# Head groups of a windowed attention: the second pass over the scores is made again by TensorE with keys on partitions, in place of transposing the exponentials

## The chip, the cores and the metric

One core of one Trainium2 chip runs the whole layer as one program. The metric is the device time of one execution in microseconds; lower is better. All data are fp32 in HBM; products that need two operands split into a high and a low part run in the fp32r format, the others in full fp32.

## The reference, cut to what matters

The layer has an attention over 1024 latent tokens with 8 query heads and 2 key/value heads (4 query heads share one key/value head), head width 64. A block of 128 queries reads one softmax over a per-head sink logit, 256 context keys and the latent keys within 128 positions.

```python
s_loc = jnp.einsum("bqhgd,bkhd->bhgqk", qb, kb).astype(jnp.float32) * scale
s_loc = jnp.where(valid, s_loc, NEG_INF)
s_ctx = jnp.einsum("bqhgd,bkhd->bhgqk", qb, k_ctx).astype(jnp.float32) * scale
p = jax.nn.softmax(jnp.concatenate([sink_col, s_ctx, s_loc], axis=-1), axis=-1)
o = (jnp.einsum("bhgqk,bkhd->bqhgd", p[..., 1:1 + n_ctx], v_ctx)
     + jnp.einsum("bhgqk,bkhd->bqhgd", p[..., 1 + n_ctx:], vb))
```

Beside it there is a Conformer convolution (31 taps, 512 channels) with a layer norm, and a vector `mod = silu(c) @ w_mod + b_mod`, of which sections 2 to 5 are needed only after the attention. The attention's and the convolution's outputs feed `w_out`; then comes the gated MLP.

## The kernel before, in words

The program is two blocks one after the other. The first makes the norms, the input projection, the convolution and the attention; the second makes the output projection and the MLP. Each engine has its queue written out by hand in program order, and semaphores join them.

The input projection for queries, keys and values runs over `NK` = 10 tiles of 128 tokens (2 of context, 8 latent). Queries and keys are normed and rotated on DVE, split into a high and a low half (`qst`, `kst`) and transposed by TensorE (`turn_qk`), so that the 128 partitions hold 64 high and 64 low rows of a query, and a key's high (or low) part twice. One product of a query with the key's high part and one with its low part give the exact score. The key is scaled by its inverse norm (`k_scaled`); the query's inverse norm `msq` is not put into the query but into the exponential's `scale`.

The attention runs over `NGRP` = 16 head groups n, each a block of 128 queries (i = n // 2) times one key/value head (4 query heads). A group has 5 key tiles of 128 keys (2 context, 3 latent), and 4 at the two edges (groups 0, 1, 14, 15). So there are 76 items (n, j). The scores and maxima run one group ahead of the rest, and a group goes so:

- `scores(n + 1, hl)` on TensorE, one head at each of the first four items of group n: queries on partitions, 640 keys along the columns; a context product of 256 columns with the high and one with the low key part, the same for two latent tiles, a mask by an identity product, and the third latent tile likewise with its mask: 8 products for a head of an inner group. It waits for the exponential of the head two before, which frees its two PSUM banks.
- `maxima` on DVE: `reduce_max` over 640 columns (L1274) and a small `tensor_scalar` (L1277) that scales it and takes the sink in.
- `exps` on ACT (L990): exponential of 640 columns, with the sum of a row into `accum_out`.
- `turn(n, j)` on TensorE (L728): four transposes of 128 x 128, one for each head, into bank 4 or 5.
- ACT copies that bank to SBUF (`pt`, L1059).
- `values(n, j - 1)` on TensorE (L740): two full-fp32 products of 256 columns, one for even and one for odd heads, each writing 64 of the 128 PSUM partitions of bank 6.
- `denominators` on DVE (sum plus sink, reciprocal of 4 columns), `spread` on TensorE (L752: four products that lay the reciprocals out over 64 partitions), a copy on ACT (L1068), and one multiplication on DVE (L1419) that ends the group.

Around this stand the convolution's taps on DVE (`taps`, `join_taps`, groups 1 to 9), the layer norm (groups 10 to 15, with TensorE's `mean`, `variance`, `broadcast`, `column_sums` in `beside`), the split of `w_out` (`WO_HIGH`, `WO_LOW`), and the second modulation on GpSimd: for 8 row blocks and 4 sections it multiplies a loaded 128 x 1024 piece of `w_mod` by a column (L546) and adds it into `sums` by an accumulating DMA (L554). GpSimd starts this after the last transposed key or query is placed (`qkT_out`). `row_sums` (L800) are the last products of the block.

## Time and profile before

| what | value |
|---|---|
| median of 3 runs | 1178.93 us (1176.92 to 1184.31) |
| profiled execution | 1178.23 us; span 1176.4 us, mean granted TensorE clock 0.988 |
| TensorE busy in the span | 1114.9 us (95%) |
| DVE, ACT, POOL busy | 935.4, 581.5, 288.0 us |
| HBM traffic | 113.26 MB read, 30.41 MB written |

The span runs from the first to the last profiled instruction; the execution's own time is 1.8 us longer. An engine's busy share is an average over stages with different limits, so the stage of the head groups (about 228 to 422 us from the span's start) is read by itself below. A matmul's own duration contains its pipeline's depth; what it costs in a stream is the distance from its start to the next one's start.

### The profile page before, as it was taken

Reading aid. Unit: us, or ns where it says so; the run is one execution under the profiler, and the core shown is the slowest. Engines: PE = TensorE matmul, PEld = TensorE weight load, DVE = VectorE, ACT = ScalarE, POOL = GpSimd, SP = SyncE. Lnnn points to the kernel's source line nnn. Section 1 sums busy time; section 2 is a strip of 40 time slices with the busy share of each in tenths; the row PEclk is TensorE's granted clock in tenths of the full one; section 3 lists DMA queues with packets and bytes.
Section 4 is the critical chain, followed back from the end, with each engine's and each line's share of the span. In section 5 each row is a group of like instructions: output and inputs, shape, how many; then the busy total and the mean of one; then the engine's idle time right before and its main releaser. Section 6 shows DMA issues by size and latency. Waiting matters only on the chain.

```text
span 1176.4 us, 16722 instructions
## 1 busy us (share of the span) xinstructions
PE 1114.9 (95%) x5745; PEld 908.1 (77%) x5745; DVE 935.4 (80%) x1430; ACT 581.5 (49%) x1007; POOL 288.0 (24%) x329
## 2 busy tenths in 40 slices
PE   7899999889878899998899999999999999999998
PEld 7787888767656677876688888878888878888886
DVE  0679988787988664469999999999999875868776
ACT  1662356865646775555443434343534444444442
POOL 2200111134464000002545544555520020000010
PEclk9999999998999899999999999999999999999999
DMA  9422556629999315222445353545342375354354
GB/s 365 163 80 73 119 107 118 151 48 257 255 243 270 93 55 178 91 77 84 147 140 180 125 181 128 178 134 178 116 152 74 123 260 196 107 118 133 99 132 109
DMA packets 103089, 171.74 MB, mean 146 GB/s; under 512 B 9323, under 2 KB 62691, under 8 KB 102005
## 3 DMA queue, kind: packets, MB, share of 16 engines
q1 hardware_dynamic: 83540, 106.79, 27.6%
q0 software_dynamic: 19488, 64.17, 22.5%
q8 instruction: 35, 0.57, 0.2%
q14 instruction: 26, 0.20, 0.1%
HBM read 113.26 MB, written 30.41 MB: 122 GB/s over the span
## 4 chain that ended last, share of the span: by engine, by line
PE 42%; DVE 12%; issue 5%; ACT 4%; DVEq 0%; ACTq 0%
PE ps L1711 19%; PE ps L1761 6%; PE ps L1763 6%; PE ps L1762 6%; PE ps L1676 5%; DVE y L2127 2%; DVE w_op L2028 2%; DVE w_raw L2046 1%; DVE y L2123 1%; ACT y L1920 1%; ACT w_op L1832 1%; DVE u L2116 1%; DVE s_sum L2046 1%; ACT h_second L1825 0%; PE ps L1687 0%
## 5 line engine op out<-in xcount | busy, mean ns | idle before, releaser
L1711 PE MATMUL ps<-t_op,w_op 128*128 128x512 f32 x1056 | 247.7, 390 | 3.8 <-DVE cv L2116 2.1
L1711 PEld LDWEIGHTS ps<-t_op,w_op 128*128 128x128 f32 x1056 | 197.5, 188 | 48.1 <-issue 4.9
L1711 PE MATMUL ps<-hx,w_op 128*128 128x512 f32 x792 | 189.5, 392 | 8.8 <-DVE u L2116 6.1
L1711 PEld LDWEIGHTS ps<-hx,w_op 128*128 128x128 f32 x792 | 149.1, 189 | 42.1 <-DVE u L2116 6.2
L1832 ACT ACTIVATE w_op<-w_raw 128x512 fp32r<-128x512 f32 x132 | 79.9, 623 | 195.0 <-DVE w_raw L2046 191.1
L1761 PE MATMUL ps<-dnh,ah 128*128 128x512 f32 x308 | 120.1, 390 | 1.6 <-DVE dnl L2134 1.6
L1763 PE MATMUL ps<-dnh,al 128*128 128x512 f32 x308 | 119.8, 389 | 0.0
L1762 PE MATMUL ps<-dnl,ah 128*128 128x512 f32 x308 | 119.8, 389 | 0.0
L2028 DVE TENSOR_TENSOR w_op<-w_raw,w_op 128x512 fp32r<-128x512 f32 x132 | 101.5, 783 | 10.1 <-ACT w_op L1832 8.5
L1940 ACT ACTIVATE ah<-hid 128x512 fp32r<-128x512 f32 x77 | 48.6, 632 | 116.8 <-PE ps L1763 112.7
L2134 DVE TENSOR_TENSOR al<-hid,ah 128x512 fp32r<-128x512 f32 x77 | 53.2, 691 | 46.3 <-ACT ah L1940 45.8
L2278 POOL DMA_DIRECT2D wd<-in_w_down x44 | 32.0, 728 | 236.2 <-DVE h_first L2017 162.2
L1676 PE MATMUL ps<-wo_op,hx 128*128 128x512 f32 x336 | 79.4, 392 | 0.3 <-PEq L350 0.3
L1676 PEld LDWEIGHTS ps<-wo_op,hx 128*128 128x128 f32 x336 | 62.4, 188 | 14.1 <-issue 1.1
L1761 PEld LDWEIGHTS ps<-dnh,ah 128*128 128x128 f32 x308 | 57.8, 188 | 14.3 <-DVE dnl L2134 2.4
L1763 PEld LDWEIGHTS ps<-dnh,al 128*128 128x128 f32 x308 | 57.8, 188 | 12.1
L1762 PEld LDWEIGHTS ps<-dnl,ah 128*128 128x128 f32 x308 | 57.8, 188 | 11.9
L740 PE MATMUL ps<-pt,vraw 128*64 128x256 f32 x304 | 49.9, 412 | 16.9 <-ACT pt L1059 16.8
L2284 POOL TENSOR_TENSOR wd<-wd 128x256 f32<-128x256 f32 x44 | 46.4, 1055 | 76.6 <-DMA wd<-in_w_down 74.9
L990 ACT ACTIVATE p<-ps,scal,msq 128x640 f32<-128x640 f32 (+1 forms) x60 | 51.8, 864 | 27.0 <-DVE scal L1277 25.4
L1274 DVE TENSOR_REDUCE scal<-ps 128x1 f32<-128x640 f32 (+1 forms) x64 | 50.0, 782 | 16.8 <-PE ps L711 10.7
L1059 ACT ACTIVATE pt<-ps 128x512 f32<-128x512 f32 x76 | 44.9, 592 | 21.0 <-PE ps L728 20.6
(294 smaller groups left out, 2369.4 us busy)
## 6 DMA issues: line engine op xcount, KB each, us to landing
w_raw<-in_w_up SPq DMA_DIRECT2D x44, 512.0 KB, 5.0
wm<-in_w_mod SPq DMA_DIRECT2D x32, 512.0 KB, 6.2
sums<-wm POOLq DMA_DIRECT2D x32, 512.0 KB, 8.4
wd<-in_w_down POOLq DMA_DIRECT2D x44, 256.0 KB, 3.3
w_down_sums<-wd POOLq DMA_DIRECT2D x44, 256.0 KB, 2.8
dn_raw<-w_down_sums SPq DMA_DIRECT2D x44, 256.0 KB, 2.6
hid_scratch<-hid SPq DMA_DIRECT2D x20, 512.0 KB, 4.3
hid<-hid_scratch POOLq DMA_DIRECT2D x20, 512.0 KB, 5.4
```

The source lines that it names most:

```text
L740: last = pe.matmul(ps[a * HD:(a + 1) * HD, 6, 0:2 * P], vraw[:, kts[j], g, :], pt[:, it % NPT, :].rearrange("p (r a q) -> p a r q", r=2, a ...
L990: act.activation(probs(n)[:, hl, 0:w], score_ap(hh, w), ACT.Exp, scale=msq[:, CT + n // NG, GQ * (n % NG) + hl:GQ * (n % NG) + hl + 1], bi ...
L1274: dve.reduce_max(s[:, 0, hl:hl + 1], score_ap(hh, w), axis=AX.X, negate=True).then_inc(max_done, 1)
L1676: last = pe.matmul(ps[:, b + hh, :], a, wo_half(k, lo, hh), start=(k == 0 and v == 0 and lo == 0), stop=(k == KT - 1 and v == 1))
L1711: last = pe.matmul(bank_of(p, s), w_op[p][w][:, k, :], rows_of(p, k, v), start=(start and k == 0 and w == 0 and v == 0), stop=(k == KH - 1 ...
L1761: pe.matmul(o, ah[b][:, c_], dnh[b][:], start=start, stop=False, skip_group_check=True)
L1762: pe.matmul(o, ah[b][:, c_], dnl[b][:], start=False, stop=False, skip_group_check=True)
L1763: return pe.matmul(o, al[b][:, c_], dnh[b][:], start=False, stop=(i == NK2 - 1), skip_group_check=True)
L1832: act.activation(w_op[p][0][:], w_part(s, p), ACT.Copy).then_inc(up_hi, 1)
L1940: act.activation(ah[n % 3][:], down_rows(p, i), ACT.Copy).then_inc(dn_hi, 1)
L2028: dve.tensor_tensor(out=w_op[p][1][:], in0=w_part(s, p), in1=f(w_op[p][0][:]), op=ALU.subtract).then_inc(up_lo, 1)
L2134: dve.tensor_tensor(out=lo[n % 3][:], in0=src, in1=f(hi[n % 3][:]), op=ALU.subtract).then_inc(dn_split, 1)
```

## The change

- The first pass over the scores is made only for the row maxima: `scores` leaves out the low part of the keys (5 products in place of 8 for a head of an inner group) and waits for the maximum of the head two before, not for its exponential.
- A second pass, `turned_scores(n, j)`, takes the transposes' place: the 128 keys of a tile are stationary, the 4 heads' queries (512 columns) move, once with the key's high and once with its low part; a masked tile has one more product of 512 columns; and a last one of 512 columns adds minus the row maximum (`onesr` stationary; `shift`, a diagonal of 128 x 128 for each head, moving).
- ACT makes the exponential of those 512 columns straight into `pt`; the exponentials of 640 columns, their accumulated sums and the copies of `pt` are gone.
- `values` comes two items later (`LAG` = 2), and makes the sums of the exponentials by two more full-fp32 products of 256 columns with `ones` as the stationary operand, into columns 256 to 511 of the same bank; the sink's term goes in by four small products at a group's last item. `spread` and `rden`'s copy are gone.
- `normalized(n)` on DVE: a reciprocal of 256 columns from PSUM, and the multiplication. It stands at item j = 1 of the next group. `shifts(n + 1)` on DVE makes the minimum with the sink, the diagonal (512 columns) and the sink's argument at item 3; `maxima` loses its small second instruction. The bank of the output alternates between 6 and 7 for groups 3 to 9 (`out_bank`).
- In the tiles of the input projection each latent tile's queries are scaled by `msq` on DVE (`q_scaled`, 512 columns) before the split.
- GpSimd starts the second modulation after the last tile of the input projection (`qkv_mm`), with `sums` at another place in SBUF; the places of `w_out`'s halves are permuted, and ACT no longer waits for the modulation before the first of them.

```diff
-        sums = [at(kib, f"sums{a}", [P, D]) for a, kib in enumerate((83, 87, 91, 95))]
-        pbuf = [at(119, "p0", [P, GQ, SW]), at(129, "p1", [P, GQ, SW])]
+        sums = [at(kib, f"sums{a}", [P, D]) for a, kib in enumerate((123, 127, 131, 135))]
+        shift = at(119, "shift", [P, 2, GQ, P], F32R)
+        neg_max = at(17.75, "neg_max", [P, 2, GQ], F32R)
+        onesr = at(17.25, "onesr", [P, P], F32R)
...
-        WO_KIB = ((57, 61), (65, 69), (99, 103), (73, 77), (81, 85), (89, 93), (107, 111))
+        WO_KIB = ((81, 85), (89, 93), (99, 103), (73, 77), (57, 61), (65, 69), (107, 111))
...
+        def out_bank(n):
+            return 7 if n % 2 and 3 <= n < LN else 6
+
+        LAG = 2
+        item_of = [(n, j) for n in range(NGRP) for j in range(len(key_tiles(n // NG)))]
...
-                pool.wait_ge(qkT_out, len(items))
+                pool.wait_ge(qkv_mm, NK)
...
                     if hh >= 2:
-                        pe.wait_ge(exp_done, hh - 1)
+                        pe.wait_ge(max_done, hh - 1)
...
-                    pe.matmul(ps[:, b, 0:CTX], q, kTc[:, g, 0, :], start=True, stop=False)
-                    pe.matmul(ps[:, b, 0:CTX], q, kTc[:, g, 1, :], start=False, stop=True)
-                    o = ps[:, b, CTX:CTX + 2 * P]
-                    pe.matmul(o, q, kl[0][:, lat:lat + 2 * P], start=True, stop=False)
-                    last = pe.matmul(o, q, kl[1][:, lat:lat + 2 * P], start=False, stop=False)
+                    pe.matmul(ps[:, b, 0:CTX], q, kTc[:, g, 0, :], start=True, stop=True)
+                    last = pe.matmul(ps[:, b, CTX:CTX + 2 * P], q, kh[:, lat:lat + 2 * P], start=True, stop=False)
...
-                    for hl in range(GQ):
-                        last = pe.transpose(ps[:, pt_bank(it), hl * P:(hl + 1) * P], probs(n)[:, hl, j * P:(j + 1) * P], ident[:])
-                    last.then_inc(pt_T, 1)
...
+                        pe.wait_ge(exp_done, it - 1)
+                    o = ps[:, st_bank(it), :].rearrange("p (h q) -> p h q", h=GQ)
+                    q = hx[:, GQ * g:GQ * (g + 1), 0, i * P:(i + 1) * P]
+                    for v in range(2):
+                        if kt < CT:
+                            k_ = kTc[:, g, v, kt * P:(kt + 1) * P]
+                        else:
+                            k_ = hx[:, 2 * g + v, 1, (kt - CT) * P:(kt - CT + 1) * P]
+                        pe.matmul(o, k_, q, start=(v == 0), stop=False)
+                    if kt >= CT and kt - CT != i:
+                        mask = mask_prev if kt - CT < i else mask_next
+                        pe.matmul(o, mask[:], identr[:].unsqueeze(1).to_broadcast([P, GQ, P]), start=False, stop=False)
+                    if j == 0:
+                        pe.wait_ge(shift_done, n + 1)
+                    pe.matmul(o, onesr[:], shift[:, n % 2], start=False, stop=True).then_inc(st_mm, 1)
...
+                    if j == 0 and n:
+                        pe.wait_ge(o_norm, n if out_bank(n - 1) == b else n - 1)
...
+                    pe.wait_ge(exp_done, it + 1)
+                    first, end = (j == 0), (j == len(kts) - 1)
+                    if end:
+                        pe.wait_ge(sexp_done, n + 1)
+                        for hl in range(GQ):
+                            r, a = divmod(hl, 2)
+                            pe.matmul(ps[a * HD:(a + 1) * HD, b, (2 + r) * P:(3 + r) * P], st[n % 2][:, 3, hl:hl + 1].to_broadcast([P, HD]), ident[:],
+                                      start=False, stop=False, skip_group_check=True)
+                    probs = pt[:, it % NPT, :].rearrange("p (r a q) -> p a r q", r=2, a=2)
+                    for c_, w in enumerate((vraw[:, kts[j], g, :], ones[:, 0:HD])):
+                        for a in range(2):
+                            last = pe.matmul(ps[a * HD:(a + 1) * HD, b, 2 * c_ * P:2 * (c_ + 1) * P], w, probs[:, a],
+                                             start=first and c_ == 0, stop=end, skip_group_check=True)
                     last.then_inc(pv_mm, 1)
...
+                def exps(it):
+                    act.wait_ge(st_mm, it + 1)
+                    if it >= NPT:
+                        act.wait_ge(pv_mm, it - NPT + 1)
+                    act.activation(pt[:, it % NPT, :], ps[:, st_bank(it), :], ACT.Exp).then_inc(exp_done, 1)
...
+                    if m >= CT:
+                        q3 = h3(qa[:, m % 2, :])
+                        dve.tensor_tensor(out=q3, in0=q3, in1=msq[:, m, 0:NH].unsqueeze(2).to_broadcast([P, NH, HD]), op=ALU.mult).then_inc(q_scaled, 1)
...
+                def shifts(n):
...
+                    dve.tensor_tensor(out=neg_max[:, n % 2], in0=s[:, 0, :], in1=sinks[:, 1, GQ * g:GQ * (g + 1)], op=ALU.min).then_inc(negm_done, 1)
+                    dve.wait_ge(negm_done, n + 1)
+                    dve.tensor_tensor(out=shift[:, n % 2], in0=ident[:].unsqueeze(1).to_broadcast([P, GQ, P]),
+                                      in1=f(neg_max[:, n % 2]).unsqueeze(2).to_broadcast([P, GQ, P]), op=ALU.mult).then_inc(shift_done, 1)
+                    dve.tensor_tensor(out=s[:, 3, :], in0=sinks[:, 0, GQ * g:GQ * (g + 1)], in1=f(neg_max[:, n % 2]), op=ALU.add).then_inc(arg_done, 1)
...
+                def normalized(n):
+                    b = out_bank(n)
+                    dve.wait_ge(pv_mm, first_item[n + 1])
+                    dve.reciprocal(rden[:], ps[:, b, 2 * P:4 * P]).then_inc(den_done, 1)
+                    dve.wait_ge(den_done, n + 1)
+                    if n:
+                        dve.wait_ge(o_lo, n)
+                    dve.tensor_tensor(out=on[:], in0=ps[:, b, 0:2 * P], in1=rden[:], op=ALU.mult).then_inc(o_norm, 1)
```

## Rows read from the trace of the kernel before

**Rows 1.** The page, part 2: tenths of TensorE's full clock in 40 slices of 29.4 us

```profile
PEclk9999999998999899999999999999999999999999
```

**Rows 2.** Windows: busy us (x instructions) of PE, PEld, DVE, ACT, POOL; clock; DMA

```profile
226.00:250.00 24.00, 19.08 (x142) 15.18 (x141) 16.12 (x43) 18.17 (x42) 0.00 (x0) 0.86 0.27 94
...
300.00:325.00 25.00, 22.23 (x179) 16.38 (x179) 22.68 (x42) 14.72 (x34) 11.59 (x13) 1.00 1.02 250
325.00:350.00 25.00, 17.93 (x146) 12.70 (x146) 22.15 (x37) 14.23 (x31) 15.89 (x13) 1.00 1.00 243
```

**Rows 3.** Timeline of DVE (start us, us): ends of groups 1 and 12

```profile
252.84 0.42 DVE L1419 TENSOR_TENSOR on<-ps,rden 128x256 f32<-128x256 f32 x1
...
392.90 0.42 DVE L1419 TENSOR_TENSOR on<-ps,rden 128x256 f32<-128x256 f32 x1 [0.16 <-PE ps L740]
```

**Rows 4.** Waits, 226 to 426 us: us in total, times, longest

```profile
ACT p L990 <- DVE scal L1277: 25.4, 32, 2.6
PEld ps L740 <- ACT pt L1059: 23.0, 16, 4.1
...
PEld ps L698 <- ACT p L990: 9.8, 18, 1.5
```

**Rows 5.** Timeline of PE: one head's scores, four transposes, two value products

```profile
301.98 0.36 PE L698 MATMUL ps<-kTc,hx 128*128 128x256 f32 x1
302.19 0.28 PE L699 MATMUL ps<-kTc,hx 128*128 128x256 f32 x1
302.30 0.29 PE L701 MATMUL ps<-hx 128*128 128x256 f32 x1
...
302.54 0.22 PE L704 MATMUL ps<-mask_prev,identr 128*128 128x128 f32 x1
302.60 0.28 PE L709 MATMUL ps<-hx 128*128 128x128 f32 x1
...
302.83 0.28 PE L711 MATMUL ps<-mask_next,identr 128*128 128x128 f32 x1
302.94 0.63 PE L728 MATMUL ps<-ident,p 128*128 128x128 f32 x4
303.50 0.65 PE L740 MATMUL ps<-pt,vraw 128*64 128x256 f32 x4
304.08 0.39 PE L698 MATMUL ps<-kTc,hx 128*128 128x256 f32 x1
```

**Rows 6.** Timeline of PE in the input projection: an fp32r product of 512 columns

```profile
150.73 0.40 PE L826 MATMUL ps<-qwh,hx 128*128 128x512 f32 x1
150.96 0.28 PE L827 MATMUL ps<-qwh,hx 128*128 128x256 f32 x1
```

**Rows 7.** Timeline of PE: full-fp32 products late in the stage, and its end

```profile
411.66 0.66 PE L752 MATMUL ps<-ident,scal 128*64 128x128 f32 x8
412.14 1.03 PE L740 MATMUL ps<-pt,vraw 128*64 128x256 f32 x8
413.11 1.09 PE L728 MATMUL ps<-ident,p 128*128 128x128 f32 x8
414.58 1.94 PE L791 MATMUL ps<-ones,sums 128*128 128x32 f32 x16 [0.38 <-DVE cacc L1300]
...
421.95 3.70 PE L800 MATMUL ps<-sums,ones 128*128 128x512 f32 x8
```

**Rows 8.** Timeline of PE: where the first and the second group start

```profile
230.95 1.09 PE L728 MATMUL ps<-ident,first_probs 128*128 128x128 f32 x4 [2.19 <-DVE ka L1209]
...
241.48 0.39 PE L698 MATMUL ps<-kTc,hx 128*128 128x256 f32 x1
```

**Rows 9.** DVE by source line: ns min/median/max, first and last start us, forms

```profile
L1993 DVE RECIPROCAL scal<-scal x8: 164/164/165, 452.0 to 527.9; 128x1 f32<-128x1 f32 x8
L1293 DVE RECIPROCAL scal<-scal x1: 195/195/195, 405.0 to 405.0; 128x8 f32<-128x8 f32 x1
L1260 DVE TENSOR_TENSOR qst<-qa,qst x8: 681/683/693, 167.7 to 240.2; 128x512 fp32r<-128x512 f32 x8
```

**Rows 10.** Lines, 226 to 426 us: busy us, mean ns of one | idle before

```profile
L1277 DVE TENSOR_SCALAR scal<-scal,msq,sinks 128x1 f32<-128x1 f32 x60 | 16.4, 273 | 2.2
```

More of the change, by code:

```diff
@@ L736, in values @@
                     if j == 0 and n == 0:
                         pe.wait_ge(qkT_out, IN_GROUPS)
-                    pe.wait_ge(pt_out, it + 1)
-                    for a in range(2):
-                        last = pe.matmul(ps[a * HD:(a + 1) * HD, 6, 0:2 * P], vraw[:, kts[j], g, :],
-                                         pt[:, it % NPT, :].rearrange("p (r a q) -> p a r q", r=2, a=2)[:, a],
-                                         start=(j == 0), stop=(j == len(kts) - 1), skip_group_check=True)
@@ L743, in values @@
-                    last.then_inc(pv_mm, 1)
-                def spread(n):
-                    pe.wait_ge(den_done, 2 * n + 2)
-                    if n < 2:
-                        pe.wait_ge(qkT_out, IN_GROUPS + 3 * (n + 1))
-                    bank_read(n)
-                    for hl in range(GQ):
-                        r, a = divmod(hl, 2)
-                        last = pe.matmul(ps[a * HD:(a + 1) * HD, 7, r * P:(r + 1) * P], st[n % 2][:, 2, hl:hl + 1].to_broadcast([P, HD]), ident[:],
-                                         start=(r == 0), stop=True, skip_group_check=True)
-                    last.then_inc(r_mm, 1)
+                    if j == 0 and b == 7:
+                        pe.wait_ge(qkT_out, len(items))
@@ L846, in _ @@
                         beside(n, j)
-                        if j == OUT_AT(n):
-                            spread(n)
-                        if j:
-                            values(n, j - 1)
-                    values(n, m - 1)
+                        if first_item[n] + j >= LAG:
+                            values(first_item[n] + j - LAG)
+                for it in range(len(item_of) - LAG, len(item_of)):
+                    values(it)
                 for r in range(2):
@@ L1010, in beside @@
                     if k is not None:
-                        if k == 0:
-                            for a in range(NW):
-                                act.wait_ge(mod_acc[a], 16 * KT)
-                        elif k > 1:
+                        if k > 1:
                             act.wait_ge(ln_mm, 4 if k == 2 else 6)
@@ L1023, in _ @@
                         placed += 1
-                    if m == NK - 2:
-                        for hl in range(2):
-                            exps(0, hl)
                     read_tile(m)
@@ L1034, in _ @@
                         product(act)
-                        for hl in range(2, GQ):
-                            exps(0, hl)
                         place(placed)
@@ L1341, in _ @@
                             maxima(0, hl)
+                        shifts(0)
                     square_sums(m)
@@ L1364, in _ @@
                     i, g, kts = head_steps(n)
-                    s = st[n % 2]
-                    dve.wait_ge(negm_done, GQ * (n + 1))
-                    dve.tensor_tensor(out=s[:, 3, :], in0=sinks[:, 0, GQ * g:GQ * (g + 1)], in1=s[:, 1, :], op=ALU.add).then_inc(arg_done, 1)
                     for j in range(len(kts)):
@@ L1370, in _ @@
                             maxima(n + 1, j)
+                            if j == GQ - 1:
+                                shifts(n + 1)
+                            if n and j == 1:
+                                normalized(n - 1)
                             if n == 0 and j == 0:
@@ L1410, in _ @@
                             wo_split_low(dve, WO_LOW[n, j])
[L1411 to L1413 removed]
+                        if n == NGRP - 1 and j == 1:
+                            normalized(n - 1)
+                        if n and j == 3:
                             output_low(n - 1)
[L1415 to L1419 removed]
+                normalized(NGRP - 1)
                 modulation()
```

101 lines of the change are left out of this document (29 added, 72 removed).

## The prediction

> **What bounds the kernel now.** I read the clock's strip first: it is at full speed nearly everywhere, with dips inside the attention stage [rows 1]. Then the stage by windows: TensorE is busy 22.2 of 25 us in one window and 17.9 in the next, DVE 22.7 and 22.2, and ACT and GpSimd are far below [rows 2]. At the start the clock is 0.86, after TensorE has sat idle. So neither TensorE nor DVE is full, and the waits say why: ACT's exponential waits for DVE's scaled maximum (25.4 us in all), TensorE's values for ACT's copy of `pt` (23.0 us on the weight loads alone), and its scores for the exponential (9.8 us) [rows 4]. It is a ring through three engines: scores, maximum, exponential, next scores. Last, the pace: group 1 ends at 252.84 and group 12 at 392.90, so a group of five tiles takes 140.06 / 11 = 12.73 us [rows 3].
>
> How much of that is TensorE's own work? I go by distances from start to start. A head's scores: 301.98 to 302.94, 0.96 us. Four transposes: 302.94 to 303.50, 0.56. An item's values: 0.58 [rows 5]. The spread of the reciprocals: 411.66 to 412.14, 0.48 [rows 7]. A group: 4 x 0.96 + 5 x 0.56 + 5 x 0.58 + 0.48 = 10.0 us, plus 0.25 on the mean for the layer norm. So TensorE waits some 2.5 us of each group, a fifth. The question is whether what the change gives TensorE to do is less than what it frees.
>
> **TensorE, part by part.** First pass: an inner head keeps its first product (0.21), one more of 256 columns (0.12), a mask (0.06), one of 128 (0.11) and its mask (0.11): 0.61 us in place of 0.96 [rows 5]. An edge head keeps three: 0.39.
>
> Second pass: a tile takes 3 products of 512 columns (high, low, shift), and 4 where it is masked, 5 x 3 + 2 = 17 in a group of five tiles and 4 x 3 + 1 = 13 in one of four. An fp32r product of 512 columns takes 150.73 to 150.96, 0.23 us [rows 6]: 3.9 us, where the transposes took 2.8.
>
> Values: four full-fp32 products of 256 columns in place of two. The stretch at 412.14 has just these eight records (two items' worth) and lasts to 413.11: 0.97 us an item [rows 7], where it was 0.58. Even and odd heads write different halves of the array's columns and already run side by side, so the sums by ones queue behind the values. The sink's products are those of the spread, 0.45.
>
> A change of kind between the second pass and the values costs about 0.1: four transposes at 0.11 each (the step from 302.83 to 302.94) would be 0.44 and take 0.56 [rows 5]. In all 4 x 0.61 + 3.9 + 5 x 0.97 + 0.5 + 0.45 = 12.1 us a group, 12.4 with the layer norm. That is as long as the 12.73 us that a group takes now. **The waits go, and TensorE's own work takes their place.**
>
> **The whole stage.** From the start of group 1's first item to the end of the values TensorE has: first pass 48 x 0.61 + 8 x 0.39 = 32.4; second pass, 13 + 12 x 17 + 2 x 13 = 243 products x 0.23 = 55.9; values 74 x 0.97 = 71.8 (two items come over from group 0, as they now lag by two); changes of kind 74 x 0.1 = 7.4; sinks 16 x 0.45 = 7.2; three sets of key and query transposes, at 0.44 each, 1.3; the unchanged work beside, 8 records of 512 columns at (3.70 - 0.6) / 7 = 0.44 and 48 small ones at 0.12, 9.3 [rows 7]. Sum 185.3 us.
>
> Group 0: TensorE is held to 230.95 by DVE's rotation of the last tile, which frees a score bank, and this wait stays; from there to group 1 it takes 10.53 us [rows 8] for 6.6 us of work at full clock (three sets of transposes, four items of values, a spread, two heads, two key and query sets). The new work there is 10 x 0.23 + 2 x 1.07 + 2 x 0.39 + 0.9 = 6.1 us. With the same waits and slow clock, group 1 starts at 241.0, 0.5 earlier.
>
> So the values end at 241.0 + 185.3 = 426.3 if TensorE never waits, against 421.95 now (where L800 starts) [rows 7]. Waits that I expect to stay: where the output has one bank (groups 1, 2 and 11 to 15), the next values need the normalized output, which is a reciprocal and a multiplication after the last values, while TensorE has only a head and a second pass (0.61 + 0.92 = 1.5 us) to fill it; seven times 0.3. And the layer norm's mean and variance now stand behind the normalization in DVE's queue: 2 us in groups 11 and 12. Together about 4: the values end near 430, 8 us later than now.
>
> **DVE.** The reciprocal of 256 columns is in no row. One column takes 164 ns and eight 195 [rows 9]: 4.4 ns a column, so 164 + 255 x 4.4 = 1.29 us; the other end is the 0.42 us of the multiplication of the same width from PSUM [rows 3]. I take 1.29, since both reciprocals' rows set it. A group loses four L1277 at 0.27 [rows 10] and two small instructions, 0.35, and gets the minimum (0.16), the diagonal (0.68, as L1260 of that width) and the reciprocal in the small one's place: +0.7. At 22.68 of 25 us [rows 2] a group of taps costs it 10.5 to 11 us now, so 11.5: under TensorE's 12.1, with little left. The scaling of the queries is another 0.68 us for each of 8 tiles in the input projection; TensorE has no wait for DVE there, the transposes come a tile later, and I put it at nothing (if that cover failed, at most 8 x 0.68 = 5.4 us). The shift is ready a tile and a half before its product asks for it.
>
> The rule of the Trainium skill that speaks against this part is in "VectorE: DVE Perf Modes", First, the fixed hardware budget: the reciprocal is an iterative divide with a repeat count of 8. At eight of its cycles a column my estimate by that page would be 2.3 us, and the seven one-bank groups would wait a microsecond longer each; the rows' 4.4 ns a column are half of that.
>
> **ACT, GpSimd, DMA, the end.** ACT drops from about 7.5 to 4 us a group and bounds nothing; an item's exponential has two items of TensorE's work to hide in. The modulation on GpSimd starts some 20 us earlier and ends as much earlier; nobody waits for its end now (the column sums at 414.58 wait for DVE [rows 7]), so it is worth nothing, and its slowing of DVE only moves to earlier groups. At the end the reciprocal, the multiplication and two small instructions (2.1 us) lie under three `row_sums` of 0.9. Nothing there.
>
> Profiled execution 1178.2 (span 1176.4 and 1.8 around it), which is the median within 0.7. Plus 8: **1186 us**.
>
> **The rivals.**
> - **DVE sets the pace (slower).** Place: the normalization at item 1 of the next group, in DVE's queue behind taps and joins, or layer-norm work. It decides where reciprocal and multiplication end more than 1.5 us after the values. For it: DVE's 90% now, its +0.7, its stretched instructions beside GpSimd. Against: seven groups have two banks. With 1.5 us lost in each of the seven one-bank groups, where I took 0.3, and 0.5 in the other nine: +13, 1199. By the page's eight cycles it comes here too.
> - **Switches and the clock come out better (no change).** If no change of kind costs anything (-7.4) and group 0 is 2 us shorter because its waits go: 1177. For it: TensorE's queue is never dry now. Against: the 0.56 for four transposes.
> - **The sums by ones are nearly free (faster).** If the array ran them beside the values, 74 x 0.39 = 29 us less: 1157. Against: the 0.97 of rows 7, where four products of two items do follow one another.
> - **The waits don't go.** If TensorE still waited a tenth of its time, +18: 1204. For it: three engines still hang together through maximum, shift and normalization. Against: all of them have more than an item of lead.
>
> **How the numbers follow.** Chances: forecast 0.50 (1181 to 1193), DVE 0.17, better switches 0.17, free sums 0.07, waits stay 0.09. The range leaves out the free sums and the far end of the last: 1168 to 1205. A measurement of this kernel tells about 1% (12 us) from no change: faster than 1167, the free sums and a little, 0.09; slower than 1191, DVE, the waits and a tenth of the forecast, 0.31; within, 0.60.
>
> **What the profile of the changed kernel would show.** TensorE busy over 24 of each 25 us from 250 to 400; distances of 0.23 for the second pass and 0.97 for an item's values; the clock at 1.00; a group each 12.4 us; reciprocals of 1.3 us; ACT half idle, waiting for TensorE; the modulation's last DMA near 360. I am wrong if the group's pace is 11 us (a distance mis-sized), or if TensorE's waits for DVE add to over 10 us.

## The result, and the profile after

| | before | changed |
|---|---|---|
| median | 1177.93 us (4 runs beside the others) | 1206.55 us (4 runs) |
| ratio | | 1.0234, 95% interval 1.0183 to 1.0285 |
| start of the first projection product | 143.8 | 145.2 |
| last projection product | 226.4 | 229.0 |
| group 1 starts | 241.48 | 243.15 |
| `row_sums` start (the values have ended) | 421.95 | 449.26 |
| span | 1176.4 us | 1204.6 us |

The changed kernel is 28.6 us slower, outside my range of 1168 to 1205. (One of its four executions, 1298 us, had a lower clock throughout and is left out of the ratio, as is one of 1434 us of the first experiment.) The 27.3 us at `row_sums` are all but 0.9 us of the difference between the spans. Of them 1.7 are there when group 1 starts, and 25.6 come in groups 1 to 15.

The page of the changed kernel: the span, part 1, and part 2's clock, which answers to [rows 1]; below, ACT's exponentials in part 5.

```profile
span 1204.6 us, 16655 instructions
...
PE 1157.0 (96%) x5825; PEld 917.4 (76%) x5825; DVE 962.1 (80%) x1390; ACT 519.9 (43%) x861; POOL 289.7 (24%) x330
...
PEclk9999999899999999999999999999999999999999
...
L987 ACT ACTIVATE pt<-ps 128x512 f32<-128x512 f32 x76 | 45.4, 597 | 137.8 <-PE ps L736 137.8
```

ACT now waits 137.8 us for TensorE: the ring of before [rows 4] is cut, as meant. The windows of the changed kernel, columns as in [rows 2]:

```profile
250.00:275.00 25.00, 23.79 (x164) 15.29 (x164) 22.45 (x31) 6.77 (x14) 10.16 (x11) 1.00 1.04 261
275.00:300.00 25.00, 25.00 (x170) 15.55 (x168) 22.06 (x30) 6.77 (x14) 14.27 (x14) 1.00 1.04 263
300.00:325.00 25.00, 25.00 (x170) 15.85 (x170) 23.73 (x29) 6.84 (x14) 14.04 (x14) 1.00 1.05 260
325.00:350.00 25.00, 25.00 (x170) 15.66 (x168) 24.79 (x36) 6.92 (x14) 13.50 (x12) 1.00 1.03 252
350.00:375.00 25.00, 22.65 (x149) 14.10 (x145) 22.53 (x28) 5.88 (x13) 6.53 (x6) 1.00 0.79 214
375.00:400.00 25.00, 21.81 (x130) 12.96 (x128) 15.90 (x24) 8.80 (x17) 0.00 (x0) 0.93 0.00 1
400.00:425.00 25.00, 23.30 (x144) 14.57 (x144) 14.70 (x26) 8.96 (x15) 0.00 (x0) 0.93 0.07 22
425.00:450.00 25.00, 23.81 (x166) 15.70 (x167) 17.14 (x25) 8.58 (x16) 0.00 (x0) 1.00 0.20 65
```

From 275 to 350 TensorE never stops, and DVE comes up to 24.79 of 25 us beside it: one full engine and one close to it. Over the 200 us TensorE is busy 190.4, so it still waits 9.6. And two windows have a clock of 0.93, which is 2 x 25 x 0.07 = 3.5 us lost (3.4 by the two stretches at the lower clock themselves). The kernel before lost more to the clock in the same stage. Its windows from 250 us on that are not at 1.00:

```profile
250.00:275.00 25.00, 22.00 (x172) 16.59 (x170) 22.63 (x40) 15.55 (x34) 14.98 (x16) 0.93 0.72 162
275.00:300.00 25.00, 22.20 (x167) 16.25 (x164) 21.11 (x38) 15.70 (x36) 13.01 (x13) 0.93 1.03 257
350.00:375.00 25.00, 22.25 (x153) 15.69 (x153) 19.34 (x37) 14.10 (x31) 11.33 (x12) 0.93 1.04 261
375.00:400.00 25.00, 22.61 (x158) 16.65 (x160) 15.63 (x33) 17.05 (x38) 4.63 (x5) 0.86 0.65 176
```

So the time from the start of group 1 to `row_sums` divides into three parts: TensorE's gaps, what the lower clock cost (half the time that TensorE ran at it), and the rest, which is its own work at full clock.

| us | length | gaps | lower clock | own work |
|---|---|---|---|---|
| before | 180.5 | 23.1 | 8.5 | 148.8 |
| changed | 206.1 | 10.1 | 3.4 | 192.6 |

The change took away 13 us of waits and 5 us of lower clock, and put 44 us of work in their place. One item of the changed kernel in the timeline of TensorE, against [rows 5]:

```profile
366.13 0.38 PE L699 MATMUL ps<-kTc,hx 128*128 128x256 f32 x1
366.36 0.28 PE L700 MATMUL ps<-hx 128*128 128x256 f32 x1
366.47 0.22 PE L702 MATMUL ps<-mask_prev,identr 128*128 128x128 f32 x1
366.53 0.27 PE L707 MATMUL ps<-hx 128*128 128x128 f32 x1
366.65 0.27 PE L708 MATMUL ps<-mask_next,identr 128*128 128x128 f32 x1
366.75 0.68 PE L730 MATMUL ps<-hx 128*128 128x512 f32 x2
367.27 0.39 PE L733 MATMUL ps<-identr,mask_prev 128*128 128x512 f32 x1
367.50 0.39 PE L736 MATMUL ps<-shift,onesr 128*128 128x512 f32 x1
367.81 0.65 PE L759 MATMUL ps<-pt,vraw 128*64 128x256 f32 x4
368.30 0.60 PE L759 MATMUL ps<-pt,ones 128*64 128x256 f32 x4
368.83 0.39 PE L699 MATMUL ps<-kTc,hx 128*128 128x256 f32 x1
```

A head's first pass is 366.13 to 366.75, 0.62 us. The second pass's two products of queries take 0.52 together, by their single records 0.285 and 0.23; the mask 0.23. From `shift`'s product to the values there are 0.31 to 0.33, 0.1 of it the price of passing to the values. The values and sums take 367.81 to 368.83, 1.02. The same timeline where TensorE stops:

```profile
361.78 0.50 PE L736 MATMUL ps<-shift,onesr 128*128 128x512 f32 x1 [2.35 <-DVE shift L1267]
...
383.35 1.10 PE L767 MATMUL ps<-sqc,meanw 128*128 128x512 f32 x2 [1.92 <-DVE cacc L1280]
384.38 0.96 PE L759 MATMUL ps<-pt,vraw 128*64 128x256 f32 x4
385.12 1.07 PE L759 MATMUL ps<-pt,ones 128*64 128x256 f32 x4
386.13 0.58 PE L699 MATMUL ps<-kTc,hx 128*128 128x256 f32 x1
...
400.86 1.22 PE L774 MATMUL ps<-meanw,sqc 128*128 128x64 f32 x8 [2.13 <-DVE sqc L1308]
...
449.26 3.70 PE L806 MATMUL ps<-sums,ones 128*128 128x512 f32 x8
```

Three stops of about 2 us, with 0.6, 0.6, 0.85 and 1.19 at one-bank groups, make up the 9.6; one of 0.43 at 245.10 lies ahead of the first window, so the stage has 10.1, all of it waiting for DVE. After the second stop the item at 384.38 takes 1.75 us, not 1.02: the clock has gone to its lower level, 1.2 GHz. What DVE does before the first and before the second stop, in its timeline:

```profile
353.78 2.97 DVE L274 SCALAR_TENSOR_TENSOR cacc<-u,cols,cacc 128x1024 f32<-128x1024 f32 x1
...
358.01 2.05 DVE L274 SCALAR_TENSOR_TENSOR cacc<-u,cols,cacc 128x1024 f32<-128x1024 f32 x1
359.99 0.81 DVE L1256 TENSOR_REDUCE scal<-ps 128x1 f32<-128x640 f32 x1
360.83 0.16 DVE L1265 TENSOR_TENSOR neg_max<-scal,sinks 128x4 fp32r<-128x4 f32 x1
361.03 0.69 DVE L1267 TENSOR_TENSOR shift<-ident,neg_max 128x512 fp32r<-128x512 f32 x1
...
379.80 1.76 DVE L1350 RECIPROCAL rden<-ps 128x256 f32<-128x256 f32 x1 [1.38 <-PE ps L759]
381.59 0.42 DVE L1354 TENSOR_TENSOR on<-ps,rden 128x256 f32<-128x256 f32 x1
381.93 1.27 DVE L1280 TENSOR_TENSOR cacc<-cacc,ps 128x512 f32<-128x512 f32 x2
```

At 361.03 the shift for group 10 comes right behind the joins (L274, the `join_taps` of the convolution), with no gap before any row from 353.78 to 361.03. The two joins took 2.97 and 2.05 us, where the nine of this kernel have a median of 1.28: 2.5 us more together, as much as the stop of 2.35. GpSimd was at work on the modulation, multiplying or issuing a DMA, beside 2.94 us of the one and 1.76 us of the other. In the thirteen traces of this case no join over 1.4 us stands without GpSimd beside it (15 of them), though most that have it beside them (76) are not stretched.

At 379.80 DVE starts the normalization, for which TensorE does not wait yet, and the layer norm's subtraction of the mean, for which it does, stands behind its 2.2 us. The reciprocal takes 1.76 us; the one of four columns that it replaced took 0.18.

### The profile page after: what moved, and what is told of

Its sections match the earlier page's. It is cut to its first block, busy times and chain, and to the rows that moved or that the text cites. A ratio compares the mean times of both kernels' runs of the same rounds, so it can differ in the third digit from the quotient of the medians.

```text
span 1204.6 us, 16655 instructions
## 1 busy us (share of the span) xinstructions
PE 1157.0 (96%) x5825; PEld 917.4 (76%) x5825; DVE 962.1 (80%) x1390; ACT 519.9 (43%) x861; POOL 289.7 (24%) x330
## 4 chain that ended last, share of the span: by engine, by line
PE 36%; DVE 14%; issue 6%; ACT 5%; DVEq 0%; ACTq 0%
PE ps L1702 14%; PE ps L1752 5%; PE ps L1753 5%; PE ps L1754 5%; PE ps L1667 5%; DVE y L2118 3%; DVE w_op L2019 3%; DVE w_raw L2037 2%; ACT w_op L1823 2%; DVE y L2114 2%; ACT y L1911 1%; DVE u L2107 1%; DVE s_sum L2037 1%; ACT h_second L1816 0%; PE ps L1678 0%
## 5 line engine op out<-in xcount | busy, mean ns | idle before, releaser
L1823 ACT ACTIVATE w_op<-w_raw 128x512 fp32r<-128x512 f32 x132 | 79.9, 623 | 194.8 <-DVE w_raw L2037 192.6
L987 ACT ACTIVATE pt<-ps 128x512 f32<-128x512 f32 x76 | 45.4, 597 | 137.8 <-PE ps L736 137.8
L1667 PEld LDWEIGHTS ps<-wo_op,hx 128*128 128x128 f32 x336 | 62.4, 188 | 14.1 <-issue 1.1
L1754 PEld LDWEIGHTS ps<-dnh,al 128*128 128x128 f32 x308 | 57.8, 188 | 12.1
L1753 PEld LDWEIGHTS ps<-dnl,ah 128*128 128x128 f32 x308 | 57.8, 188 | 11.9
L1256 DVE TENSOR_REDUCE scal<-ps 128x1 f32<-128x640 f32 (+1 forms) x64 | 50.1, 784 | 19.4 <-PE ps L708 10.6
L549 POOL TENSOR_SCALAR wm<-wm,scal 128x1024 f32<-128x1024 f32 x32 | 43.0, 1345 | 46.4 <-DMA wm<-in_w_mod 46.2
L2275 POOL TENSOR_TENSOR wd<-wd,wd 128x256 f32<-128x256 f32 x44 | 52.5, 1192 | 3.4
```

The lines of the kernel that those rows point to most:

```text
L987: act.activation(pt[:, it % NPT, :], ps[:, st_bank(it), :], ACT.Exp).then_inc(exp_done, 1)
L1256: dve.reduce_max(s[:, 0, hl:hl + 1], score_ap(hh, w), axis=AX.X, negate=True).then_inc(max_done, 1)
L1667: last = pe.matmul(ps[:, b + hh, :], a, wo_half(k, lo, hh), start=(k == 0 and v == 0 and lo == 0), stop=(k == KT - 1 and v == 1))
L1753: pe.matmul(o, ah[b][:, c_], dnl[b][:], start=False, stop=False, skip_group_check=True)
L1754: return pe.matmul(o, al[b][:, c_], dnh[b][:], start=False, stop=(i == NK2 - 1), skip_group_check=True)
L1823: act.activation(w_op[p][0][:], w_part(s, p), ACT.Copy).then_inc(up_hi, 1)
```

## The experiments

Each kernel is the changed kernel with the edit shown. "2-8" is the mean time of groups 2 to 8 from one end (the multiplication, L1354) to the next; "9-12" and "13-15" are sums over those groups; the `row_sums` column is where they start in the profiled execution. The last three columns divide the time from the start of group 1 to `row_sums`, as above: TensorE's gaps, the cost of the lower clock, its own work. A ratio is to executions of the kernel before that ran beside that kernel (their medians lie between 1177.04 and 1178.04), so a difference between two medians of the table is good to about 1 us at best.

| kernel | median us | ratio to before, 95% | 2-8 | 9-12 | 13-15 | `row_sums` | gaps | lower clock | own |
|---|---|---|---|---|---|---|---|---|---|
| before | 1177.93 | | 11.8 | 57.4 | 29.2 | 422.0 | 23.1 | 8.5 | 148.8 |
| changed | 1206.55 | 1.0234 (1.0183-1.0285) | 12.8 | 64.0 | 34.4 | 449.3 | 10.1 | 3.4 | 192.6 |
| e1b_no_ones | 1188.84 | 1.0086 (1.0055-1.0116) | 12.0 | 57.3 | 29.1 | 430.6 | 17.7 | 10.4 | 161.7 |
| e2_copy_for_reciprocal | 1195.72 | 1.0151 (1.0114-1.0188) | 12.7 | 57.0 | 32.2 | 438.0 | 3.3 | 0 | 192.5 |
| e9_neither | 1169.81 | 0.9932 (0.9912-0.9952) | 10.6 | 51.9 | 26.6 | 411.5 | 5.8 | 3.4 | 160.6 |
| e3_no_query_scaling | 1203.15 | 1.0210 (1.0172-1.0248) | 12.8 | 62.4 | 34.4 | 445.9 | 10.5 | 3.4 | 192.6 |
| e4_norm_work_first | 1200.95 | 1.0185 (1.0144-1.0226) | 12.9 | 57.3 | 34.4 | 446.0 | 8.8 | 3.4 | 192.3 |
| e6_diagonal_on_act | 1207.13 | 1.0252 (1.0229-1.0276) | 12.8 | 60.7 | 34.4 | 445.1 | 8.9 | 1.5 | 193.2 |
| e7_norm_first_and_diagonal | 1196.90 | 1.0161 (1.0141-1.0181) | 12.8 | 54.7 | 34.4 | 439.4 | 3.9 | 0 | 192.4 |
| e8_modulation_late | 1203.46 | 1.0208 (1.0187-1.0229) | 12.8 | 63.1 | 34.4 | 449.1 | 8.0 | 5.1 | 192.1 |
| e10_sums_fp32r | 1200.46 | 1.0210 (1.0184-1.0236) | 12.4 | 58.6 | 33.1 | 439.8 | 15.6 | 5.1 | 179.6 |
| e11_all_three | 1187.22 | 1.0088 (1.0070-1.0105) | 12.0 | 52.4 | 33.1 | 427.3 | 6.4 | 0 | 179.8 |
| e12_taps_first_too | 1185.60 | 1.0076 (1.0060-1.0091) | 11.9 | 49.5 | 33.1 | 426.2 | 4.9 | 0 | 178.8 |

The first column of groups holds the first lesson: in the changed kernel these seven groups take a microsecond each more than before, 12.8 against 11.8. (0.5 of the 11.8 is the lower clock, from two stretches in those groups.) The last column holds the second: TensorE's own work is 192 to 193 us in every kernel that makes the changed kernel's products, whatever is done to DVE, ACT or GpSimd.

**Without the sums by ones** (the denominators are then only the constant that the sink's four products lay out).

```diff
-ps[...], st[n % 2][:, 3, hl:hl + 1].to_broadcast([P, HD]), ident[:],
+ps[...], ones[:, hl:hl + 1].to_broadcast([P, HD]), ident[:],
-for c_, w in enumerate((vraw[:, kts[j], g, :], ones[:, 0:HD])):
+for c_, w in enumerate((vraw[:, kts[j], g, :],)):
```

> The changed kernel without the products by ones: an item's values are two full-fp32 products as before the change, and the sink's four products lay out 1.0 (so the sums and the division's result are left out; the reciprocal still runs over 256 columns). Theory A, TensorE's own work is all that bounds the head groups: each of 76 items is 0.43 us shorter (two records of 256 columns behind each other), so 33 us less, 1174 us, and a group of five tiles takes 10.5 us where it took 12.7. Theory B, DVE is as full as TensorE there (23.7 and 24.8 of 25 us in two windows of the changed kernel): groups 3 to 9 fall only from 12.7 to about 12.2 us, the later ones by 1 to 2 us each, in all 12 to 18 us less, 1188 to 1194 us.

17.7 us less than the changed kernel, still 0.9% over before. Two products' distances of 0.216 in each of 76 items, 33 us of TensorE's work, are gone, and only half of that comes back. This is the size that theory B gave. The windows of this kernel say why:

```profile
275.00:300.00 25.00, 23.72 (x144) 14.09 (x142) 24.79 (x33) 8.17 (x17) 12.39 (x11) 1.00 1.03 254
300.00:325.00 25.00, 23.00 (x141) 13.90 (x137) 24.80 (x32) 7.38 (x15) 15.74 (x15) 1.00 1.03 256
...
375.00:400.00 25.00, 22.89 (x115) 14.55 (x114) 15.72 (x27) 10.05 (x21) 0.00 (x0) 0.81 0.00 1
```

Now DVE is the full one, 24.8 of 25 us, and TensorE waits for it. Its gaps grow from 10.1 to 17.7 us (5.6 of them for `shift`), and the lower clock costs 10.4 us in place of 3.4, as the windows behind the waits show (0.81 in one). So the sums are far from free, but of what they give back about 8 us go to waits for DVE and 7 to the clock.

**A copy in place of the reciprocal** (the output is multiplied by its sum, not divided).

```diff
-dve.reciprocal(rden[:], ps[:, b, 2 * P:4 * P]).then_inc(den_done, 1)
+dve.tensor_copy(rden[:], ps[:, b, 2 * P:4 * P]).then_inc(den_done, 1)
```

> The changed kernel with a copy of the 256 columns from PSUM in place of the reciprocal of them (the division is left out; the products are all made). The copy should take 0.42 us, the reciprocal took 1.76. Theory A: TensorE bounds, so groups 3 to 8 stay at 12.7 us, and only where the output has one bank or a layer norm product waits behind the normalization is something won, 7 times 0.3 to 0.8 us: 2 to 6 us less, 1201 to 1205. Theory B: DVE is the bound in groups 3 to 9 as well, and 1.3 us less of it in each of 16 groups gives 12 us or more: 1194 or less.

10.8 us less: the pace stays as theory A has it, but the gain is more than its 2 to 6. Its windows, and its row of L1350 with ns min/median/max:

```profile
275.00:300.00 25.00, 25.00 (x170) 15.61 (x166) 19.96 (x31) 6.40 (x15) 13.17 (x13) 1.00 1.01 256
300.00:325.00 25.00, 25.00 (x170) 15.70 (x166) 20.81 (x32) 6.64 (x14) 15.25 (x15) 1.00 1.05 263
```

```profile
L1350 DVE COPY rden<-ps x2: 424/424/425, 310.9 to 323.6; 128x256 f32<-128x256 f32 x2
```

DVE has 4 to 5 us of air in a window, and the pace doesn't move: groups 3 to 8 take 12.7 each, all alike. That is TensorE's own work with nobody to wait for, and it shows what bounds these groups in the changed kernel: TensorE, not DVE. The gain lies elsewhere: groups 9 to 12 lose 7 us of waits and of lower clock (3.4 of it clock, which is at 1.00 from 250 to 425 here), the one-bank groups 13 to 15 another 2.3.

**Both together.**

> The changed kernel with both relieved: no products by ones (the sink's products lay out 1.0) and a copy of 256 columns in place of the reciprocal; the sums and the division are left out. Alone the first gave 18 us and the second 11. Theory B, TensorE and DVE both full at 12.7 us a group: together they give more than the sum of the two in groups 2 to 9, where the group should fall to 10.9 to 11.2 us; in all 32 to 40 us less than the changed kernel, 1167 to 1175 us, which is below the kernel before. If TensorE alone bounded, it would be at most 18 + 3 = 21 us less, 1186.

36.7 us less than the changed kernel, where the two alone gave 17.7 and 10.8, together 28.5. Each hid some of the other, and the groups say where. In groups 2 to 8 the sums' removal alone gives 0.8 us a group, the copy alone 0.1, both 2.2. TensorE sets the pace there at 12.7, DVE stands at 12.0, and an edit that moves TensorE below 12.0 gets nothing more until DVE is moved too. From group 9 on the two gains nearly add up (13.7 apart and 12.1 together in groups 9 to 12, 7.5 and 7.8 in 13 to 15). The 10.6 us a group are 12.7 less 5 x 0.43. Only without either is the kernel faster than before, by 0.7%, and it does not compute the layer.

**Without the queries' scaling** (queries go unscaled by their inverse norm).

```diff
-dve.tensor_tensor(out=q3, in0=q3, in1=msq[:, m, 0:NH]..., op=ALU.mult).then_inc(q_scaled, 1)
```

> The changed kernel without DVE's scaling of the queries by their inverse norm in the tiles of the input projection (that factor is left out of the scores). Theory A: the scaling pushed the low halves of tile 3 behind the transposes that TensorE wants (its one stop of 1.2 us near 177 us) and the end of the input projection by 2.6 us in all; without it 1.2 to 2.6 us less, 1204 to 1205. Rival: the projection's later end comes from before that stage (it already starts 1.4 us later), and nothing changes within 1 us.

(The waits that hung on the scaling now go by the rotation; nothing else differs.) The projection's products take 81.4 us, against 83.8 in the changed kernel and 82.6 before, and a stop of 0.9 us in them is gone. The median is 3.4 us lower, within the two intervals' width; the projection's 1.2 us over before (2.4 against this run) is what I take as the scaling's price. The same trace answers another question. Both joins ahead of group 10 are unstretched in it, and the stop for the shift is 0.77 us in place of 2.35:

```profile
352.27 1.27 DVE L274 SCALAR_TENSOR_TENSOR cacc<-u,cols,cacc 128x1024 f32<-128x1024 f32 x1
354.99 1.27 DVE L274 SCALAR_TENSOR_TENSOR cacc<-u,cols,cacc 128x1024 f32<-128x1024 f32 x1
...
358.42 0.50 PE L736 MATMUL ps<-shift,onesr 128*128 128x512 f32 x1 [0.77 <-DVE shift L1263]
```

So about 1.6 us of that stop went with the stretched joins, and whether they are stretched differs from one profiled run to the next, though GpSimd's work is the same. No run holds the rest fixed and moves the joins alone, so the 1.6 us is a comparison of two runs.

**The layer norm's work ahead of the normalization**, in groups 11 and 12: the normalization goes from before the beside work of item 1 to behind it.

```diff
-if n and j == 1:
+if n and j == 1 and n not in (LN + 1, LN + 2):
     normalized(n - 1)
...
-if n == NGRP - 1 and j == 1:
+if n in (LN + 1, LN + 2, NGRP - 1) and j == 1:
     normalized(n - 1)
```

> The changed kernel with DVE's layer norm work at item 1 of groups 11 and 12 ahead of the normalization in its queue (nothing left out). TensorE's two long waits, 1.9 us before the second mean and 2.1 us before the first variance, are for that work, and after each its clock is at half for some 4 us. Theory A: both waits go, with the slow stretches behind them: 6 to 8 us less, 1199 to 1201, since the values of the same item wait for a normalization that DVE can begin only then anyway. Rival: TensorE waits the same time one product later, for the normalization (reciprocal and multiplication, 2.2 us): 1 us or less is won.

Groups 11 and 12 take 13.6 and 13.9 us, from 17.3 and 17.9. In DVE's timeline of this kernel the order is turned:

```profile
380.24 1.28 DVE L1280 TENSOR_TENSOR cacc<-cacc,ps 128x512 f32<-128x512 f32 x2 [0.77 <-PE ps L767]
...
382.71 1.28 DVE L1280 TENSOR_TENSOR cacc<-cacc,ps 128x512 f32<-128x512 f32 x2
384.18 1.76 DVE L1350 RECIPROCAL rden<-ps 128x256 f32<-128x256 f32 x1 [0.18 <-PE ps L759]
```

TensorE is busy 25.00 of 25 us from 375 to 400, at a clock of 1.00. Both waits and the two stretches at the lower clock behind them are gone, and so they were this order, 7.7 us. The median fell by 5.6, just under the 6 to 8 of theory A; in the profiled run groups 1 and 9 were each about 1 us longer, group 9 with a stretch at the lower clock that the changed kernel's run does not have there.

**The diagonal on ACT** in place of DVE, four copies of the identity with `neg_max` as scale.

```diff
+def diagonal(n):
+    act.wait_ge(negm_done, n + 1)
...
+    for hl in range(GQ):
+        ins = act.activation(shift[:, n % 2, hl], ident[:], ACT.Copy, scale=f(neg_max[:, n % 2, hl:hl + 1]))
+    ins.then_inc(shift_done, 1)
...
-dve.tensor_tensor(out=shift[:, n % 2], ...).then_inc(shift_done, 1)
```

> The changed kernel with the diagonal of the shifts made by ACT (four activations of 128 columns, about 0.3 us each) in place of DVE (one instruction of 0.69); nothing left out. DVE is 0.6 us emptier in a group, ACT is at 28% there. Theory B: in groups 2 to 9 TensorE stays full, so they keep 12.7 us, but the wait of 2.4 us for the shift in front of group 10 goes, and DVE's lateness after the joins with it: 2 to 5 us less, 1202 to 1205. Rival: the shift now comes later, since it hangs on ACT's exponentials too, and TensorE waits at the start of each group: 5 us more or worse.

No gain in the median (1207.13, its runs from 1202.66 to 1209.86), though in the profile, which is of the 1202.66, TensorE's wait for the shift fell from 2.35 to 0.7 and group 9 from 15.3 to 13.6. But that can't be put down to this edit: both joins are unstretched here (1.28 and 1.27 us), and with such joins the run without the queries' scaling has a stop of 0.77 with the diagonal still on DVE. By itself this run is inconclusive. **With the edit before it:**

> Both orders together: the layer norm work ahead of the normalization in groups 11 and 12, and the diagonal on ACT; nothing left out. If the two savings are of different waits, they add up: 6 + 3 = 9 us less than the changed kernel, 1197 us. It is still about 20 us above the kernel before, since TensorE's own work of 12.7 us a group is untouched by either.

1196.90, 4.0 under the order alone and 9.7 under the changed kernel, as expected in size. How much of the 4.0 is the diagonal is not shown: in the profiled run of the order alone one of the two joins was stretched (2.95 us, a stop of 2.36), in this one neither was (a stop of 0.70).

**The second modulation as late as before.**

```diff
-pool.wait_ge(qkv_mm, NK)
+pool.wait_ge(qkT_out, len(items))
```

> The changed kernel with GpSimd's second modulation starting again when the last key and query are placed, as before the change (some 20 us later). Nothing is left out. Forecast's view: the place in time is worth nothing, within 1 us. Theory B: GpSimd's multiplications stretch DVE's instructions, and DVE is full in the groups of taps; later they reach less into groups 0 and 1, and more into the layer norm groups 9 to 11: the time of the groups moves, by 1 to 3 us in all, to the slower side if the layer norm chain is hit.

3.1 us less by the medians, but `row_sums` start no earlier (449.1) and the profiled execution (1207.17) is no shorter: group 9 took 12.8 us and group 12 19.4. In group 9 neither join was stretched and TensorE did not stop for the shift at all; in group 12 the lower clock held twice as long as in the changed kernel's run. I count this as no proven effect of the later start.

**The sums as fp32r products.** `pt` is written as fp32r, the values read it as before, and a sum is one product of all 128 columns with a stationary operand that is one for the heads' own half and zero for the other.

```diff
-ps[a * HD:(a + 1) * HD, b, 2 * c_ * P:...], ones[:, 0:HD], probs[:, a]
+for a in range(2):
+    last = pe.matmul(ps[:, b, 2 * P:4 * P], half_ones[a][:], probs[:, a],
+                     start=False, stop=end, skip_group_check=True)
```

> The changed kernel with the sums by ones in fp32r: ACT writes the exponentials rounded to fp32r (the values use the same rounded numbers, in full fp32), and two fp32r products of 256 columns, stationary ones in one half of the columns and zeros in the other, take the place of the two full-fp32 ones. An item should be 0.24 us of sums where it was 0.43, 1.0 us a group of five. Nothing else is left out. TensorE alone as bound: 76 x 0.2 = 15 us less, 1191. TensorE and DVE both full: groups 3 to 8 fall by less than half of that (DVE stays at some 12.2 us), 6 to 10 us less in all, 1197 to 1200.

6.1 us less, where TensorE alone would have given 76 x 0.2 = 15: the undisturbed group falls to 11.7, but DVE, whose work is as before, comes late in others: groups 5 and 6 end after 13.0 and 13.9, TensorE waits 0.25, 0.61 and 1.21 us for it between 316 and 332, and the gaps of the stage grow from 10.1 to 15.6. **All three together** take DVE's part away as well:

> The sums in fp32r, the layer norm work ahead of the normalization, and the diagonal on ACT together. DVE is then at 11.6 and TensorE at 11.7 us a group. Both bounds are moved together, so the gains should add up to more than apart: 9 us of the two orders, 12 to 15 of the sums: 1182 to 1186 us, within 1% of the kernel before, and more likely above it than below.

1187.22, 19.3 us less than the changed kernel: more than the 9.7 and 6.1 of its parts together, less than the 20.6 to 24.6 that I expected. **And groups 3 to 10** also do the work beside them at item 1 (the taps, in group 10 the layer norm's) ahead of the normalization:

```diff
-if n and j == 1 and n not in (LN + 1, LN + 2):
+if n and j == 1 and not 3 <= n <= LN + 2:
```

> As the one with all three, and in groups 3 to 10 DVE's taps of item 1 stand ahead of the normalization, which it can't begin before TensorE's last values anyway (those groups have two banks, so nobody waits for it). If DVE is the later of the two in those groups, its 0.5 to 0.8 us of waiting a group goes: 2 to 4 us less than with three edits. If TensorE is, nothing changes within 1 us.

1185.60, 21 us less than the changed kernel and still 0.8% over before. Against the run before it the 1.6 us are within the intervals. Group 9 is down to 12.0 from 14.0, with the stop for the shift gone. TensorE in this kernel:

```profile
344.65 0.65 PE L767 MATMUL ps<-pt,vraw 128*64 128x256 f32 x4
345.23 0.51 PE L770 MATMUL ps<-pt,half_ones 128*128 128x256 f32 x2
345.57 0.28 PE L706 MATMUL ps<-kTc,hx 128*128 128x256 f32 x1
```

Values and sums take 0.92 in place of 1.02, and the next head starts in fp32r right away and is 0.1 shorter (345.57 to 346.10). TensorE is at 25.00 of 25 us in every window from 275 to 375, and its groups take as long as before's with their waits: 178.8 us of own work and 4.9 of gaps at full clock, against 148.8, 23.1 of gaps and 8.5 of lower clock. No version that computes the whole layer was found that beats the kernel before.

## Why the prediction was wrong

The direction and the mechanism were right: more than half of TensorE's waits went, and its own work took their place and more. The step that failed is the sum. I had the end of the values at 430.3, and it is 449.26, 19.0 later (0.9 more comes behind it):

| term | predicted | measured | off by |
|---|---|---|---|
| start of group 1 | 241.0 | 243.15 | 2.2 |
| TensorE's own work from there | 185.3 | 192.6 | 7.3 |
| TensorE's waits | 4 | 10.1 | 6.1 |
| clock at its lower level | 0 | 3.4 | 3.4 |

(192.6 is 449.26 - 243.15 = 206.1, less 10.1 and 3.4; it comes out between 192.1 and 193.2 in all six other runs that make the same products.)

- **"12.1 us a group": mis-sized by 0.6, the largest of the four.** The second pass with its changes of kind sums to 67.3 us by the distances at full clock, where I had 55.9 + 7.4 = 63.3; the values to 73.9, where I had 71.8; the sinks' products to 7.7, where I had 7.2; the first pass to 32.8, where I had 32.4. The rest is right within 0.2. In an item, the second pass's first product takes 0.285 us behind products of 128 columns and 0.34 behind the values, not 0.23, and the values take 1.02, not 0.97. I had priced a stream of unlike products by the distances in streams of like ones. The 0.05 I could have seen: the two pairs of [rows 5] take 0.58, not half of 0.97, since a first pair takes 0.26 to the next where others take 0.21, and 0.58 with two more steps of 0.216 is 1.01.
- **"That is as long as the 12.73 us that a group takes now": the wrong yardstick.** 12.73 is a mean that held the layer norm's and the joins' groups; groups 2 to 8 alone took 11.8. No term of the sum used it, but a plain group of 12.1 set against 11.8 would have shown that the change loses even there.
- **"So TensorE waits some 2.5 us of each group": part of it was the clock.** Of the 31.6 us that the kernel before spent beside TensorE's own work from group 1 on, 8.5 were the lower clock. There were 23.1 us of waits to win, for 44 us of work.
- **"So 11.5: under TensorE's 12.1" (DVE): the order held, the size did not.** The reciprocal of 256 columns takes 1.76 us, 6.2 ns a column, not 1.29. The slope from 1 to 8 columns did not hold at 256. The page "VectorE: DVE Perf Modes" of the Trainium skill, section First, the fixed hardware budget, gives the repeat count of 8 from which I had 2.3 us; the trace lies midway between the two. With 0.47 more DVE's 11.5 becomes 12.0, which is the pace of the run without the sums, where DVE is full. DVE was busy 24.79 of 25 us in one window, and once it was late: TensorE waited 2.35 us for `shift`, which I had "a tile and a half" early. The run with the copy prices the reciprocal at 10.8 us in the layer.
- **Layer norm, "2 us in groups 11 and 12": 7.5.** The waits are 1.92 and 2.13, each about the length of the normalization in front, and I left out that TensorE can go on at half the clock after such a stop: 3.4 us more. That part varies from run to run: the same two stops had 6.8 us at the lower clock behind one of them without the queries' scaling, and none behind the second with the diagonal on ACT. The experiment that turns the order took both stops away.
- **One-bank groups, "seven times 0.3" = 2.1:** four waits with 3.2 us in all. Right in place, and near in size.
- **Queries' scaling, "at nothing":** the projection became 1.2 us longer, with one stop. The other 1.4 us are there before its first product, where nothing is changed; across all runs that start lies between 143.8 and 146.4.
- **Group 0, "0.5 earlier":** right in sign. From the last projection product to group 1 it is 14.2 us, 15.1 before.
- **Modulation, "worth nothing":** its place in time, as far as the runs can tell. Its last DMA was issued at 359.3, near the 360 predicted. But "its slowing of DVE only moves to earlier groups" failed: with DVE near its limit, the two joins stretched beside GpSimd go with about 1.6 of the 2.35 us that TensorE stopped ahead of group 10.

Of the rivals, "DVE sets the pace" (1199) had the place of most waits right, in the one-bank and the layer norm groups, but DVE does not set the pace of the plain groups: with the copy they keep their 12.7 us. "The waits don't go" (1204) was nearest in number, but its 18 us were to be waits, and there are 10.1; the work of 7.3 us and the clock's 3.4 are in no rival. One of my signs of being wrong came true: TensorE's waits for DVE add to 10.1 us, just over 10. "TensorE busy over 24 of each 25 us from 250 to 400" held in three windows of six.

## What to carry to other kernels

Before a plain stretch of the new schedule is compared with the old, take out of the old mean the groups that carry other work. When a change loads the bounding engine and the one just under it at once, price the pair: here an edit that relieved one alone gave about half of the work that it took away, and both together more than their sum. Split what looks like waiting into gaps and lower clock before counting it as time to win. Work that nobody waits for does not belong in a queue ahead of work for which the bounding engine waits, and a stop of 2 us there cost nearly twice its length where the clock fell after it. A small difference between two single profiles needs a look at the instructions that another engine can stretch before an edit is credited with it.

## What the runs showed of the hardware that I had not expected

- A reciprocal of 256 fp32 columns from PSUM: 1757 ns, 6.2 ns a column, against 4.4 from 1 to 8 columns.
- An fp32r product of 512 columns behind products of 128 columns: 0.285 us to the next start, where the next ones take 0.229.
- From the last pair of values or sums to whatever comes next with all 128 columns stationary: 0.309, where a pair is followed by another at 0.21. It is no price of the number format alone: the kernel before has 0.310 from its values to full-fp32 transposes (412.80 to 413.11, the end of the stretch in [rows 7]). Moving the sums to fp32r moved this step between values and sums, and did not remove it.
- A join of 128x1024 on DVE: 1.28 us, and up to 2.97 with GpSimd at work beside it. Many that had GpSimd beside them took 1.28 all the same; what decides between the two was not tried.
- After stops of 1.92 and 2.13 us the clock was at 1.2 GHz, until 388 and 405 us; after 2.35 us at 361.78 it was not: the values and sums behind it took 1.01 us (362.21 to 363.22). In the run with the norm work first it was, behind 2.36 us at the same place (its window from 350 to 375 has 0.93). What decides between the two was not tried.
